# Two model blocks on one core: order of a value GEMM, pieces of the layer norms, steps of the gated attention

## The chip, the cores and the metric

One of the eight cores of a Trainium2 chip runs the whole program; the other cores stand idle. The metric is device time in microseconds (us), median of several executions. Engines: TensorE (PE, with its weight load PEld), VectorE (DVE), ScalarE (ACT), GpSimd (POOL), SyncE (SP, which issues most DMAs).

## What is computed

A sequence of 512 tokens, 1024 wide, runs through a first block (block-sparse attention beside gated linear attention, GLA, then a squared-ReLU MLP) and through two layers of a second block:

```python
# second block, per layer: deepnorm residuals around an attention and an MLP
proj = x @ w_in;  fq, fk, fv, f_logit, rq, rk, rv, rg = split(proj)
fox_out = fox_attention(fq, fk, fv, log_sigmoid(f_logit + b))       # softmax heads
ret = retention(rotary(rq), rotary(rk), rv);  ret = groupnorm(ret)  # 4 heads of 128
x = layernorm(ALPHA * x + concat(fox_out, silu(rg) * ret) @ w_out)
x = layernorm(ALPHA * x + relu(x @ w_ff1)**2 @ w_ff2)
```

All inputs are f32. Products are made of three fp32r products: each operand is split into a high and a low part.

## The kernel before

Activations lie transposed: eight tiles of 128 features by 512 tokens (`H`; split copies `P` and `Q`, each `hi` and `lo`). Weights stream from HBM in slabs into two stage buffers; `prepare()` (L253) turns one piece of 1024 columns into `wh` on ACT (L269) and `wl` on DVE (L270). `piece()` (L279) hands out the next piece and prepares ahead of it, as long as a ring slot is free. A GEMM of one piece (`gemm`, L309) is eight k steps of three matmuls (L298, L300, L301) of 512 tokens into one of four rotating PSUM banks; `gemm_tok` (L359) computes values with tokens on the partitions and goes over the four banks in turn.

Each engine runs its instructions in the order in which the Python program emits them, so that order is the schedule. Attention work is emitted in between: `tick()` (L410) follows every k step and adds `pace[0]`; at each whole number, one step of the generator at the head of `background` runs. The softmax generator (L666) takes two steps for each of 32 score tiles and calls `chore()` (L387) once in every pair; chores are small pieces of work put off by others. The rotary evacuation `ev_r` (L1483) puts off two chores for each tile, `first_half` (L1488, L1491) and `second_half` (L1496, L1499), and its bank counts as owed until the second has run. `settled(b)` (L391) runs chores until a bank's debt is gone. In a layer of the second block twelve GEMMs (L1505: rotary tiles 0 to 7 and the remaining query and key tiles) come before the value GEMM `gemm_tok(P, ev_rv)` (L1576), whose evacuation centres the values (L1511, L1513). The retention generator follows the softmax; its head 0 multiplies scores by `accq`, heads 1 to 3 by `x_dec` (L1550), which a DMA behind a reload of `H` brings (L1521, L1522).

In GLA, `gla()` (L916) runs beside 16 GEMMs of 8 ticks at a pace of 0.52. `gates(hd)` computes the decays; after the first gates three steps pass before the product L929. Three steps before the mean L992, two squares are added on DVE (L988).

`last_three` (L1257) computes the last three output tiles (5, 6, 7) ahead of a layer norm, in two halves of 256 tokens (`part(p, half, ks)`), while the norm of the first half, A, begins. `norm.late(j)` adds a tile to the running sum `accq` (L1202) and its squared deviation to `acc2`. `mean()` (L1217) and `scale()` (L1231) are matmuls with constant weights. `minus` (L1226) subtracts the mean, `times` (L1241, L1244) scales, `lows` (L1253) makes the low parts on DVE. `head(half, ks)` are the first k steps of the first three GEMMs of the next stage, by halves; the fourth GEMM comes whole after them. It is called four times: before both MLPs of the second block (LN1 of layers 0 and 1), between the layers, and at the end (`nxt` is None there: no next GEMM, and finished tiles go out by DMA).

A wait names an engine's counter and a value. `mean()` waits for `norm.acc`, the token of the last `accq` addition emitted so far, whichever half that one was for.

Of the kernel before, what the change touches and what calls it, by code (L numbers as in the profile page):

```python
# [93 lines left out]
def build(nc, xT, w_in, gate_up, w_bm, w_bg, w_out, w_up, w_down, w_in2, w_out2, w_ff1, w_ff2,  # L94
          consts, params, out, vrev, cneg):
    ctx = ExitStack()
    with ctx:
# [100 lines left out]
        for L in range(2):  # L198
# [7 lines left out]
            pair_cols(w_in2[L], 3)  # L206
            cols(w_in2[L], 1928, 2568)
            values(w_in2[L], 2568, 3080)
# [8 lines left out]
        state = {"slab": 0, "prep": 0, "use": 0, "bank": 0, "ahead": 3}  # L217
# [91 lines left out]
        def gemm(x, nk, evac, more=0):  # L309
# [3 lines left out]
            for c0 in range(0, width, 128):  # L313
# [73 lines left out]
        def chore():  # L387
            if chores:
                chores.pop(0)()

# [70 lines left out]
        t_x = []  # L461
# [5 lines left out]
        c3 = V.op(lambda e: e.memset(onev[:, :], 1.0 / 256))  # L467
        c4 = V.op(lambda e: e.memset(epsc, 1e-6))
# [37 lines left out]
        def rms_scale(t_acc, rb_use=None):  # L506
# [5 lines left out]
            t = A.op(lambda e: e.activation(rB[:, :], tB[:, :], ACT.Exp, scale=-0.5), t, rb_use)  # L512
# [153 lines left out]
        def softmax_heads(heads, vv, t_v, bias_of, finished):  # L666
# [70 lines left out]

            bias_for(0)
# [25 lines left out]
            while chores:  # L764
                chore()
                yield

# [148 lines left out]
        def gla():  # L916
# [4 lines left out]
            for _ in range(3):  # L921
                yield
            for hd in range(4):
# [67 lines left out]
                yield  # L991
                tp = PE.op(lambda e: e.matmul(banks[5][:, :], onev[:, :], sq[0][:, :], start=True,  # L992
# [14 lines left out]
        pace[0] = 0.52  # L1007
# [53 lines left out]
        finish_background()  # L1061
        for j in range(8):
# [86 lines left out]
        class Norm:  # L1149
# [50 lines left out]
            def late(self, j, sl):  # L1200

                self.acc = V.op(lambda e: e.tensor_tensor(accq[:, sl], accq[:, sl], H[:, j, sl], ALU.add),  # L1202
                                t_h[j], self.acc)
                self.deviate(j, sl)

        class Half:
# [8 lines left out]
            def mean(self):  # L1215
# [496 lines left out]
```

How the kernel before makes its waits and increments, by code:

```python
    def run(self, eng):  # L85
        for need, fn, s, inc in self.ops:
            for w, v in need:
                eng.wait_ge(w.h, v)
            ins = fn(eng)
            if s:
                ins.then_inc(s.h, inc)
# [1553 lines left out]
        @block.sync  # L1645
        def _(e):
            SP.run(e)
            e.wait_ge(s_out.h, s_out.n)
```

## Time and profile before

| | us |
|---|---|
| median of 3 runs | 2123.97 (2123.3 to 2124.76) |
| profiled execution | 2123.57 |
| its span, first to last instruction | 2121.8 |
| PE busy in the span | 2055.1 (97%) |
| DVE busy, ACT busy | 1101.9 (52%), 939.3 (44%) |
| mean granted TensorE clock | 0.995 |

The page of the profile gives busy shares; the views of the trace behind it (who waited for whom, instructions in order of time, busy time of chosen stretches with the granted clock) give the stages. Matmuls overlap, so their recorded durations are longer than their distance from start to start.

### The profile page before, as it was taken

What the parts mean: (1) busy time and instruction counts of PE and PEld (TensorE: products, weight loads), DVE (VectorE), ACT (ScalarE), POOL (GpSimd) and SP (SyncE); (2) the same over time, 40 slices, a digit from 0 to 9 for tenths busy, and PEclk for the clock granted to TensorE, in tenths of its full rate; (3) what the DMA queues carried; (4) which work ended last, traced back from release to release, by engine and by line L of the source; (5) the groups of instructions that cost most, each with busy time, mean ns of one, the idle gap of its engine ahead of it and who ended that gap; (6) DMA issues with size and microseconds to landing.
All of it is one profiled execution on the core that took longest, in us unless ns stands there. A gap on an engine that the chain in (4) does not pass through costs nothing. (4 is left out here: it accounts for less than half of the span.)

```text
span 2121.8 us, 24498 instructions
## 1 busy us (share of the span) xinstructions
PE 2055.1 (97%) x9660; PEld 1691.6 (80%) x9660; DVE 1101.9 (52%) x1795; ACT 939.3 (44%) x1513; POOL 149.4 (7%) x207
## 2 busy tenths in 40 slices
PE   8999999999999999999999999999999999999997
PEld 6888778888888888777688888888777688888886
DVE  5655556565343443576486333337676476333336
ACT  5664334335232332565557243244565347243343
POOL 0000000000000000353000000000353000000000
PEclk9999999999999999999999999999999999999999
DMA  7332213333322332632323332330632323333321
GB/s 236 95 105 64 77 60 99 121 98 120 119 91 88 100 99 61 179 100 75 114 80 102 99 103 95 100 99 21 199 91 83 114 80 100 100 99 100 99 80 40
DMA packets 201519, 211.38 MB, mean 100 GB/s; under 512 B 7803, under 2 KB 181115, under 8 KB 201404
## 3 DMA queue, kind: packets, MB, share of 16 engines
q1 hardware_dynamic: 194544, 194.13, 29.2%
q0 software_dynamic: 6352, 15.24, 2.8%
q8 instruction: 77, 1.26, 0.3%
q10 hardware_dynamic: 508, 0.43, 0.1%
q14 instruction: 38, 0.31, 0.0%
HBM read 194.55 MB, written 8.95 MB: 96 GB/s over the span
## 5 line engine op out<-in xcount | busy, mean ns | idle before, releaser
L298 PE MATMUL ps<-Phi,wh 128*128 128x512 f32 (+1 forms) x1208 | 481.1, 398 | 18.9 <-DVE Plo L448 8.7
L301 PE MATMUL ps<-Phi,wl 128*128 128x512 f32 (+1 forms) x1208 | 459.3, 380 | 0.1
L300 PE MATMUL ps<-Plo,wh 128*128 128x512 f32 (+1 forms) x1208 | 458.4, 380 | 0.0
L269 ACT ACTIVATE wh<-stage 128x1024 fp32r<-128x1024 f32 (+2 forms) x253 | 261.5, 1041 | 183.9 <-PE ps L301 167.1
L270 DVE TENSOR_TENSOR wl<-stage,wh 128x1024 fp32r<-128x1024 f32 x250 | 304.6, 1223 | 66.2 <-ACT wh L269 58.5
L298 PEld LDWEIGHTS ps<-Phi,wh 128*128 128x128 f32 x1208 | 228.4, 189 | 67.0 <-issue 19.6
L301 PEld LDWEIGHTS ps<-Phi,wl 128*128 128x128 f32 x1208 | 227.7, 188 | 44.7 <-DVE wl L270 0.8
L300 PEld LDWEIGHTS ps<-Plo,wh 128*128 128x128 f32 x1208 | 228.5, 189 | 40.8 <-issue 4.1
L298 PE MATMUL ps<-Qhi,wh 128*128 128x512 f32 (+1 forms) x680 | 256.2, 377 | 0.8 <-DVE Qlo L445 0.8
L301 PE MATMUL ps<-Qhi,wl 128*128 128x512 f32 (+1 forms) x680 | 254.4, 374 | 0.0
L300 PE MATMUL ps<-Qlo,wh 128*128 128x512 f32 (+1 forms) x680 | 254.4, 374 | 0.0
L445 DVE TENSOR_TENSOR Qlo<-f,Qhi 128x512 fp32r<-128x512 f32 x96 | 66.5, 693 | 238.8 <-ACT Qhi L444 238.8
L1120 DVE TENSOR_TENSOR H<-H,ps 128x512 f32<-128x512 f32 x72 | 49.5, 687 | 222.6 <-PE ps L301 222.6
L298 PE MATMUL ps<-Qhi,wxh 128*128 128x512 f32 (+1 forms) x408 | 150.7, 369 | 0.0
L300 PE MATMUL ps<-Qlo,wxh 128*128 128x512 f32 (+1 forms) x408 | 148.9, 365 | 0.0
L301 PE MATMUL ps<-Qhi,wxl 128*128 128x512 f32 (+1 forms) x408 | 148.8, 365 | 0.0
L298 PEld LDWEIGHTS ps<-Qhi,wh 128*128 128x128 f32 x680 | 128.1, 188 | 25.3 <-ACT Qhi L444 1.6
L300 PEld LDWEIGHTS ps<-Qlo,wh 128*128 128x128 f32 x680 | 128.1, 188 | 23.6 <-issue 1.0
L301 PEld LDWEIGHTS ps<-Qhi,wl 128*128 128x128 f32 x680 | 128.0, 188 | 22.7
L269 ACT ACTIVATE wxh<-stage 128x1024 fp32r<-128x1024 f32 x86 | 89.7, 1051 | 109.2 <-PE ps L301 104.3
L298 PE MATMUL ps<-Phi,wxh 128*128 128x512 f32 (+1 forms) x336 | 129.0, 384 | 0.0
L300 PE MATMUL ps<-Plo,wxh 128*128 128x512 f32 (+1 forms) x336 | 129.0, 384 | 0.0
(301 smaller groups left out, 2921.5 us busy)
## 6 DMA issues: line engine op xcount, KB each, us to landing
stage<-in_w_ff SPq DMA_DIRECT2D x64, 1024.0 KB, 5.4
stage<-in_w_in SPq DMA_DIRECT2D x39, 1024.0 KB, 5.3
stage<-in_w_up SPq DMA_DIRECT2D x16, 1024.0 KB, 5.3
stage<-in_w_down SPq DMA_DIRECT2D x16, 1024.0 KB, 5.2
stage<-in_w_in SPq DMA_DIRECT2D x30, 512.0 KB, 5.3
stage<-in_w_out SPq DMA_DIRECT2D x12, 1024.0 KB, 5.2
stage<-in_w_bg SPq DMA_DIRECT2D x4, 1024.0 KB, 5.4
vrev<-H SPq DMA_DIRECT2D x2, 2048.0 KB, 14.9
```

What stands on the lines that cost most here:

```text
L269: t_hi = A.op(lambda e: e.activation(hi, src, ACT.Copy), st_landed[n, part], w_free[u], sem=s_whi)
L270: t_lo = V.op(lambda e: e.tensor_tensor(lo, src, hi.bitcast(F32), ALU.subtract), st_landed[n, part], t_hi, w_free[u], sem=s_wlo)
L298: PE.op(lambda e: e.matmul(o, hi[:, k, c], x.hi[:, kx, tok], start=first, stop=False), t_hi, t_x or x.t[kx], list(waits), signal=False)
L300: PE.op(lambda e: e.matmul(o, hi[:, k, c], x.lo[:, kx, tok], start=False, stop=False), signal=False)
L301: return PE.op(lambda e: e.matmul(o, lo[:, k, c], x.hi[:, kx, tok], start=False, stop=last), t_lo, sem=s_wpe, signal=last)
L445: t2 = V.op(lambda e: e.tensor_tensor(lo, src, hi.bitcast(F32), ALU.subtract), t1, t_src, x.free, after)
L1120: t_h[j] = V.op(lambda e: e.tensor_tensor(H[:, j, :], H[:, j, :], o, ALU.add), t, t_h[j])
```

## The change

- At the start, four matmuls of constants run on PE, and the squares for the first norm's sum come three tiles behind the splits.
- `put_off` holds chores back only while the softmax generator runs (`state["turns"]`); `gemm` settles its bank as `gemm_tok` does.
- The value GEMM of the second block comes after `ev_fk(3)`, before rotary tiles 3 to 7; the slabs are reordered with it. Centring becomes a chore except for the first bank. Retention waits for the rotary tile that its head needs.
- GLA has five steps ahead of L929, one step more ahead of L992, and a pace of 0.55.
- The activation table for logarithm and exponential is loaded by name ahead of the branch GEMMs.
- `last_three` runs whole parts of the B half sooner, prepares one piece more after `part(2, 0)` and takes four GEMMs of the next stage by halves. At the end, tile 7 enters the mean and the variance through one more matmul each, and tiles 2 and 5 are finished on DVE.

```diff
                 b = next_bank()
                 o = banks[b][0:m, :]
                 for k in range(nk):
-                    t = product(o, w, k, slice(c0, c0 + m), x, k, k == 0, k == nk - 1, free[b] if k == 0 else None)
+                    t = product(o, w, k, slice(c0, c0 + m), x, k, k == 0, k == nk - 1, settled(b) if k == 0 else None)
                     tick()
...
+        def put_off(*what):
+
+            chores.extend(what)
+            while chores and not state["turns"]:
+                chore()
...
+        for _ in range(4):
+            t_idle = PE.op(lambda e: e.matmul(banks[7][:, :], ones[:, :], rB[:, :], start=True, stop=True), idle, c1)
+        free[7] = rb_free[0] = t_idle
         t_acc = None
-        for k in range(8):
-            split(P, k, H[:, k, :], [t_x[k // 2], t_prm], prm[:, V_G1 + k:V_G1 + k + 1])
+        for k in range(11):
+            if k < 8:
+                split(P, k, H[:, k, :], [t_x[k // 2], t_prm], prm[:, V_G1 + k:V_G1 + k + 1])
             if k == 0:
                 prepare()
+            k -= 3
+            if k < 0:
+                continue
...
-            for _ in range(3):
+            for _ in range(5):
...
                 sq_free[1] = t
                 yield
                 yield
+                yield
                 tp = PE.op(lambda e: e.matmul(banks[5][:, :], onev[:, :], sq[0][:, :], start=True,
...
-        pace[0] = 0.52
+        pace[0] = 0.55
...
         finish_background()
+        A.op(lambda e: e.preload_act_table_set("natural_log_exp_and_others"), signal=False)
...
+            def mean(self, rest=None):
+
                 sl, n = self.sl, self.n
-                t = PE.op(lambda e: e.matmul(banks[4][:, sl], onec[:, :], accq[:, sl], start=True, stop=True),
+                t = PE.op(lambda e: e.matmul(banks[4][:, sl], onec[:, :], accq[:, sl], start=True, stop=rest is None),
                           n.acc, free[4])
+                if rest is not None:
+                    t = PE.op(lambda e: e.matmul(banks[4][:, sl], onec[:, :], H[:, rest, sl], start=False, stop=True),
+                              t_h[rest])
...
+                while rest and n.pending:
+                    _, _, s, t_s = n.pending.pop()
+                    t = PE.op(lambda e, s=s: e.matmul(banks[5][:, sl], onec[:, :], s[:, sl], start=False, stop=True), t_s)
...
+                    if not self.keep and k in (2, 5):
+                        self.fin[k] = V.op(lambda e, k=k, g=g, b=b: e.tensor_scalar(
+                            H[:, k, sl], d8[:, k, sl], g, b, ALU.mult, ALU.add), t)
+                        continue
...
+            part(2, 0, range(8))
+            norm.add()
+            if nxt:
+                prepare()
             if last_wide:
                 narrow()
+            part(0, 1, range(8))
             A_.mean()
             A_.minus(0, 1, 2, 3)
+            part(1, 1, range(4))
             A_.scale()
             A_.minus(4, 5, 6, 7)
+            part(1, 1, range(4, 8))
             A_.times(0, 1)
+            if not nxt:
+                norm.add()
+                part(2, 1, range(8), False)
+                A_.times(2, 3)
+                B_.mean(7)
+                B_.minus(0)
+                B_.scale(True)
+                A_.times(4)
+                B_.minus(1, 2, 3, 4, 5)
+                A_.times(5, 6)
+                B_.minus(6, 7)
+                B_.times(0)
+                A_.times(7)
+                out_half(0, A_.fin)
+                for k in range(1, 8):
+                    B_.times(k)
+                    out_half(1, B_.fin, k)
+                return
             A_.lows(0)
+            A_.times(2)
+            A_.lows(1)
+            A_.times(3)
             part(2, 1, range(8))
             norm.add()
+            A_.lows(2)
+            A_.times(4)
+
+            four = [(piece(1), next_bank()) for _ in range(4)]
+
+            def step(half, k, i, w, b):
+                return product(banks[b][:, half.sl], w, k, slice(0, 128), P, k, k == 0, k == 7, free[b],
+                               tok=half.sl, t_x=half.sub[k])
 
             def head(half, ks):
+                for k in ks:
+                    for (i, w), b in four:
+                        step(half, k, i, w, b)
 
             head(A_, (0, 1))
+            A_.lows(3)
+            A_.times(5)
             B_.mean()
             A_.lows(4)
+            B_.minus(0, 1, 2)
+            A_.times(6)
+            A_.lows(5)
             head(A_, (2, 3))
             B_.scale()
+            B_.minus(3, 4)
             A_.times(7)
+            A_.lows(6)
+            B_.minus(5, 6, 7)
+            A_.lows(7)
             head(A_, (4, 5, 6, 7))
             B_.times(0)
             for k in range(1, 8):
                 B_.times(k)
                 B_.lows(k - 1)
             B_.lows(7)
+            prepare()
+            prepare()
             for k in range(8):
                 t_h[k] = [A_.fin[k], B_.fin[k]]
+                P.t[k] = [A_.sub[k], B_.sub[k]]
             rb_free[0] = B_.r
             sq_free[:] = [norm.acc2, norm.acc2]
+            head(B_, range(4))
+            for ((i, w), b), ev in zip(four, nxt):
+                for k in range(4, 8):
+                    t = step(B_, k, i, w, b)
+                P.free = t
+                release(i, t)
+                if not last_wide:
                     free[b] = ev(banks[b][:, :], t)
+            for ((i, w), b), ev in zip(four, nxt if last_wide else ()):
+                free[b] = ev(banks[b][:, :], t)
...
-            for ev in (ev_r(0), ev_fq(2), ev_fk(2), ev_r(1), ev_r(2), ev_fq(3), ev_fk(3),
-                       ev_r(3), ev_r(4), ev_r(5), ev_r(6), ev_r(7)):
+            for ev in (ev_r(0), ev_fq(2), ev_fk(2), ev_r(1), ev_r(2), ev_fq(3), ev_fk(3)):
                 gemm(P, 8, ev)
             t_rv = [None] * 4
 
             def ev_rv(b, o, t):
+                box = [OWED]
+
+                def centre():
+                    box[0] = centred(b, o, t)
+                if b:
+                    put_off(centre)
+                else:
+                    centre()
+                return box
+
+            def centred(b, o, t):
                 t1 = V.op(lambda e: e.tensor_reduce(sums[:, b, :], o.rearrange("p (h d) -> p h d", h=4), AX.X, ALU.add), t)
                 total = bass.AP(tensor=sums[:, :, :].tensor, offset=4 * b, ap=[[16, 128], [1, 4], [0, 128]])
                 t_rv[b] = V.op(lambda e: e.scalar_tensor_tensor(
                     out=rv[:, b, :].rearrange("p (h d) -> p h d", h=4), in0=total, scalar=-1.0 / 128,
                     in1=o.rearrange("p (h d) -> p h d", h=4), op0=ALU.mult, op1=ALU.add), t1, Q.free)
                 return t_rv[b]
+            gemm_tok(P, ev_rv)
...
+                    while t_r[4 + h] is None:
+                        yield
...
-            gemm_tok(P, ev_rv)
+            for j in range(3, 8):
+                gemm(P, 8, ev_r(j))
```

In the body of `last_three` only the lines after the change are shown; those before it are in the function above.

## Rows read from the trace of the kernel before

**Rows 1.** The page: busy us and share (part 1); count, busy us, mean ns (part 5).
```profile
PE 2055.1 (97%) x9660; PEld 1691.6 (80%) x9660; DVE 1101.9 (52%) x1795; ACT 939.3 (44%) x1513; POOL 149.4 (7%) x207
...
L269 ACT ACTIVATE wh<-stage 128x1024 fp32r<-128x1024 f32 (+2 forms) x253 | 261.5, 1041 | 183.9 <-PE ps L301 167.1
```

**Rows 2.** Waits of PE: line, waited for, us in total, times, longest.
```profile
PE ps L370 <- DVE x_rb L1496: 10.2, 4, 3.3
PE ps L1217 <- DVE accq L1202: 8.9, 6, 2.1
...
PE ps L1547 <- DVE x_IT L1550: 5.1, 4, 2.0
PE ps L298 <- ACT H L1244: 4.7, 3, 1.6
...
PE ps L298 <- DVE Plo L1253: 3.1, 8, 0.6
PE ps L929 <- DVE kiv L911: 2.4, 1, 2.4
PE ps L992 <- DVE sq L988: 2.3, 3, 0.8
```

**Rows 3.** Timeline of PE, start: start us, duration us, instruction, [idle before <-releaser].
```profile
13.06 0.77 PE L298 MATMUL ps<-Phi,wh 128*128 128x512 f32 x1 [0.29 <-DVE Plo L448]
...
14.91 0.63 PE L300 MATMUL ps<-Plo,wh 128*128 128x512 f32 x1
15.34 0.63 PE L301 MATMUL ps<-Phi,wl 128*128 128x512 f32 x1
...
16.63 0.39 PE L298 MATMUL ps<-Phi,wh 128*128 128x512 f32 x1
...
24.11 1.02 PE L508 MATMUL ps<-accq,onec 128*128 128x512 f32 x2
```

**Rows 4.** Stretches: length, PE, PEld, DVE, ACT, POOL busy, PEclk, DMA, GB/s.
```profile
988.95:992.35 3.40, 3.40 (x9) 2.85 (x10) 0.60 (x1) 0.00 (x0) 0.00 (x0) 0.50 0.00 0
...
1736.40:1739.85 3.45, 1.36 (x12) 1.16 (x11) 2.67 (x6) 1.21 (x2) 0.00 (x0) 1.00 0.00 0
1739.90:1743.25 3.35, 3.35 (x12) 2.99 (x13) 2.44 (x8) 1.22 (x3) 0.00 (x0) 0.50 0.00 0
```

**Rows 5.** Timeline of DVE, one rotary chore of layer 0.
```profile
988.13 0.69 DVE L1496 SCALAR_TENSOR_TENSOR x_rb<-ps,x_tab 64x512 f32<-64x512 f32 x1
```

**Rows 6.** Timeline of DVE, retention of layer 0.
```profile
1027.08 1.16 DVE L1550 TENSOR_TENSOR x_IT<-ps,x_dec 128x512 f32<-128x512 f32 x2 [7.37 <-DMA x_dec<-in_consts]
```

**Rows 7.** Timeline of PE, LN1 of layers 0 and 1, and the end.
```profile
1098.18 0.28 PE L298 MATMUL ps<-Qhi,wxh 128*128 128x256 f32 x1
...
1099.14 0.28 PE L301 MATMUL ps<-Qhi,wxl 128*128 128x256 f32 x1
...
1739.78 1.16 PE L1217 MATMUL ps<-accq,onec 128*128 128x256 f32 x2 [2.09 <-DVE accq L1202]
...
2109.11 0.70 PE L1217 MATMUL ps<-accq,onec 128*128 128x256 f32 x2 [1.51 <-DVE accq L1202]
```

**Rows 8.** Timeline of DVE, LN1 of layers 0 and 1.
```profile
1101.05 0.43 DVE L1196 TENSOR_TENSOR acc<-acc,sq 128x256 f32<-128x256 f32 x1 [0.48 <-ACT sq L1187]
1101.78 1.42 DVE L1226 TENSOR_TENSOR d<-H,muB 128x256 f32<-128x256 f32 x4
...
1737.71 1.22 DVE L270 TENSOR_TENSOR wl<-stage,wh 128x1024 fp32r<-128x1024 f32 x1 [0.59 <-ACT wh L269]
```

**Rows 9.** Timelines of PE and DVE, between the layers.
```profile
1491.06 0.28 PE L301 MATMUL ps<-Phi,wxl 128*128 128x256 f32 x1
...
1492.01 1.41 DVE L603 SCALAR_TENSOR_TENSOR f0qs<-ps,f0qs 64x512 fp32r<-64x512 f32 x2 [0.99 <-ACT f0qs L602]
```

**Rows 10.** Timelines of DVE and ACT: a copy of 256 columns; the end.
```profile
222.35 0.29 DVE L901 COPY tm<-b 128x256 f32<-128x256 f32 x1
...
2115.08 4.04 ACT L1244 ACTIVATE H<-d,prm 128x256 f32<-128x256 f32 x8 [0.74 <-DVE d L1241]
```

More of the change, by code:

```diff
@@ L206, in build @@
             pair_cols(w_in2[L], 3)
+            values(w_in2[L], 2568, 3080)
             cols(w_in2[L], 1928, 2568)
-            values(w_in2[L], 2568, 3080)
             cols(w_in2[L], 3080, 3592)
@@ L216, in build @@
         w_tok, w_free, slot = {}, [None] * 7, {}
-        state = {"slab": 0, "prep": 0, "use": 0, "bank": 0, "ahead": 3}
+        state = {"slab": 0, "prep": 0, "use": 0, "bank": 0, "ahead": 3, "turns": False}
         ring_free = [0, 1, 2, 3]
@@ L1198, in add, with late @@
                     sq_free[k % 2] = self.acc2
-            def late(self, j, sl):
-                self.acc = V.op(lambda e: e.tensor_tensor(accq[:, sl], accq[:, sl], H[:, j, sl], ALU.add),
-                                t_h[j], self.acc)
+            def late(self, j, sl, summed=True):
+                if summed:
+                    self.acc = V.op(lambda e: e.tensor_tensor(accq[:, sl], accq[:, sl], H[:, j, sl], ALU.add),
+                                    t_h[j], self.acc)
                 self.deviate(j, sl)
@@ L1227, in minus, with scale @@
                                      self.t_m, t_h[k], self.n.d[k])
-            def scale(self):
+            def scale(self, rest=False):
                 sl, n = self.sl, self.n
-                t = PE.op(lambda e: e.matmul(banks[5][:, sl], onec[:, :], acc2[:, sl], start=True, stop=True),
+                t = PE.op(lambda e: e.matmul(banks[5][:, sl], onec[:, :], acc2[:, sl], start=True, stop=not rest),
                           n.acc2, free[5])
+                while rest and n.pending:
+                    _, _, s, t_s = n.pending.pop()
+                    t = PE.op(lambda e, s=s: e.matmul(banks[5][:, sl], onec[:, :], s[:, sl], start=False, stop=True), t_s)
                 t = V.op(lambda e: e.tensor_tensor(qB[:, sl], banks[5][:, sl], qB[:, sl], ALU.subtract), t, self.q)
@@ L1283, in part @@
                     release(i, t)
-                norm.late(j, sl)
+                norm.late(j, sl, then)
             part(0, 0, range(8))
@@ L1289, in last_three @@
                 prepare()
+            part(2, 0, range(8))
+            norm.add()
+            if nxt:
+                prepare()
             if last_wide:
                 narrow()
-            part(2, 0, range(8))
-            norm.add()
-            part(0, 1, range(3))
+            part(0, 1, range(8))
             A_.mean()
             A_.minus(0, 1, 2, 3)
-            part(0, 1, (3, 4))
+            part(1, 1, range(4))
             A_.scale()
             A_.minus(4, 5, 6, 7)
-            part(0, 1, (5, 6, 7))
+            part(1, 1, range(4, 8))
@@ L1302, in last_three @@
             A_.lows(0)
-            part(1, 1, range(8))
-            for k in range(2, 5):
-                A_.times(k)
-                A_.lows(k - 1)
+            A_.times(2)
+            A_.lows(1)
+            A_.times(3)
             part(2, 1, range(8))
             norm.add()
-            if nxt:
-                two = [(piece(1), next_bank()) for _ in range(3)]
-            def head(half, ks):
-                for k in ks if nxt else ():
-                    for (i, w), b in two:
-                        t = product(banks[b][:, half.sl], w, k, slice(0, 128), P, k, k == 0, k == 7, free[b],
-                                    tok=half.sl, t_x=half.sub[k])
-                        if k == 7 and half is B_:
-                            P.free = t
-                            release(i, t)
-                return t if nxt else None
+            A_.lows(2)
@@ L1622, in build @@
             last_three(norm, alpha, V_LN1G + 8 * L, V_LN1B + 8 * L,
-                       [lambda o, t, j=j: up(j, o, t) for j in range(3)])
+                       [lambda o, t, j=j: up(j, o, t) for j in range(4)])
             norm = None
-            for j in ff(up, alpha, 3, 5):
+            for j in ff(up, alpha, 4, 5):
                 if norm is None:
```

30 lines of the change are left out of this document (7 added, 23 removed).

## The prediction

> **What bounds the kernel now.** I read the page's busy shares first: PE is busy 97% of the span [rows 1], so a change can only take away waits of PE or its slow clock. Next comes the view of PE's waits [rows 2]: the large ones are the value GEMM behind rotary chores (10.2 us in two layers), the means and first heads around the layer norms (8.9, 4.7 and 3.1), retention (5.1) and GLA (2.4 and 2.3). Then I read the stretches with the granted clock [rows 4]: twice PE falls to 0.50, the 1.2 GHz level, for 3.4 us; a fall like the first also follows the same wait in layer 1. Last come the timelines around each wait. The profiled execution took 2123.57 us, its span 2121.8; the 1.8 around it stay. The median, 2123.97, is 0.4 above it.
>
> **The start.** PE runs without a gap from 13.06, behind DVE's split of tile 1 [rows 3]. The copy of the first square stands ahead of that split; moved three tiles back, it frees up to the 0.3 us that PE waits there. At first matmuls follow each other every 0.43 us (14.91 to 15.34), later every 0.227 (33 of them from 16.63 to 24.11). The 42 from 13.06 to 24.11 took 11.05 us, at full speed 42 x 0.227 = 9.5: the slow part costs 1.5. The four constant matmuls are f32, two passes each; L508 shows 0.43 a pass at full speed [rows 3], so 8 passes at half speed are 6.9 us, begun behind DVE's first memsets and done about when PE's first operand is there; before that PE has nothing to do, so they cost nothing, whatever they bring. But after them PE has only six matmuls until 13: it stands most of that time, as it did ahead of the fall at 1739.9 (1.36 us busy in 3.45) [rows 4]. So the clock may fall again. The gain lies between 0 and 1.8; I take 1.0, the middle.
> The Trainium skill, page "TensorE: Matmul & The Clock Gate", calls the slow level the default that activity releases (section "What's actually happening"); by that alone the term would be -1.8 and the forecast 2109.0. Its section "HAM oscillation — how this bites in real kernels" says that a wait between bursts brings the slow level back; by that it would be -0.3 and 2110.5. The row at 1739.9 agrees with the second.
>
> **GLA.** A step comes every 1/0.55 ticks of three matmuls, 1.82 x 0.68 = 1.24 us of PE (1.31 before). Two more steps give L929's operand 2.5 us for a wait of 2.4; one more gives L988 1.24 for waits of at most 0.8 [rows 2]. Both could go: -4.7. Every other chain loses 0.07 us a step, and what ends next to nothing today may show; I take -4.3, bounds -5 and -2.5. The steps are 65 now (59 before); 128 ticks give 70, so none is left over. The table load by name and what it moves on ACT cost nothing: no wait of PE in rows 2 lies at the Ln that it serves.
>
> **Rotary and values.** Ahead of the value GEMM four tiles' chores are owed now, and its second round of banks runs them in a burst: 10.2 us of waits, 5.1 a layer [rows 2]. The second wait ends in the fall of the clock, 3.4 us at half speed, 1.7 lost [rows 4]. Put behind `ev_fk(3)`, the value GEMM finds banks whose debts are paid: -6.8 a layer. What is late next? Chores run once in two steps, at 0.52 a tick 2.1 in a GEMM, and every tile adds two; three centrings of 1.4 us come on top. I count three chores, 3 x 1.4 = 4.2 us of DVE (two operations of 0.69 each) [rows 5], left when tile 7's GEMM ends. They stand ahead of retention's first products on DVE, where today the last centrings and the last head stand: that wait (part of L1547's 5.1 [rows 2]) stays. SP's queue moves too: the reload of `H` waits for the last chore, and `x_dec` is behind it. DVE already stands 7.37 us for `x_dec` [rows 6]; I take it 0.8 later (0 to 1.2), all of it PE's wait. Denser chores in the five GEMMs cost 0.7 in small waits (0 to 2). Net -5.3 a layer, -10.6 in all; bounds -14 and -7.
>
> **The norms before a next GEMM (three).** PE's work is the same, the fourth GEMM's in halves instead of whole: 24 more matmuls of 0.12 us (8 steps in 0.96) [rows 7] in each half. So the time moves by the sum of waits: 8.9 + 4.7 + 3.1 [rows 2] less the 1.5 at the end, 15.2 for three, 5 each; those 1.5 and the 2.09 below stand in [rows 7]. Three things speak against its going. First, `part(0, 1)` now comes whole ahead of `A_.mean()`, and `norm.acc` is then the addition of the B half's tile 5, so the mean of A waits for a number that it doesn't need. Second, the extra `prepare()` puts a 1.22 us split, behind 1.04 us for its high part on ACT [rows 1], on DVE in between; that split already made the wait of 2.09 in layer 1 [rows 8]. In LN1 of layer 0 the last sum of A starts on DVE at 1101.05 [rows 8]; the split then runs from about 1102.1 to 1103.3, tile 5's sum is ready at 1104.1, while PE, 15 matmuls after 1099.4 [rows 7], is at the mean at 1101.2: 2.9 us of wait. Third, from there DVE has some 20 operations of 0.335 (four in 1.42 [rows 8]) and the hops over ACT, about 9.5 us, until the first low part, and PE has 48 x 0.12 + 0.7 and the hop: it waits 2.2 more. With 1 in small pieces it is 6 against 5. From DVE's side, the earlier cover gives 1.4 back. I take -0.5, -0.5 and, as layer 1 already has its fall, -1.2: -2.2 in all, bounds -6 and +4.
> One new wait is sure: between the layers all four evacuations come after the last matmul, and the thin forget GEMM reuses the first one's bank. Matmuls end at about 1491.3, L603's two operations at 1493.4 [rows 9]: +2.1 (1.5 to 2.5).
>
> **The end.** The mean of A again waits for tile 5 of B, without a split: +1.1 for PE. Four finishing operations go from ACT to DVE, 0.29 (a copy of 256) [rows 10] to 0.42 each [rows 8]: +1.2 to 1.7 on the engine that is last then. The eight finishes on ACT, 4.04 us, end behind DVE's last operation today [rows 10], and that lag goes; one `accq` and one `acc2` addition (0.34 each) go too, but DVE waits for tile 7 with `times` behind it. +1.8, bounds 0 and +2.8.
>
> **Sum.** -1.0 - 4.3 - 10.6 - 2.2 + 2.1 + 1.8 = -14.2: span 2107.6, an execution like the profiled one 2109.4, the median 2109.8.
>
> **Rivals.**
> Norms pay: if tile 5's sum and the extra split fit beside PE (the split's ACT half done early), the waits fall from 5 to about 2 in each norm: -10 instead of -2.2, and the end +0.5. -1.0 - 4.3 - 10.6 - 10 + 2.1 + 0.5 = -23.3: 2100.7. For it: four GEMMs cover more than three. Against it: both lie on DVE's in-order path.
> Rotary gives part of it back: more chores are left than I count, or `x_dec` and a new fall of the clock cost 5 a layer. -2 a layer: -7.6, 2116.4. For it: DVE waits on `x_dec` already.
> The reordering doesn't do what it says: the key tile's evacuation just ahead of the value GEMM takes the place of the rotary burst, and rotary gains nothing: -3.6, 2120.4. Against it: only one bank, with 4.1 us of matmuls before it is needed.
> Slower: the burst moves to the end of tile 7's GEMM, where nothing but `step_background` stands until retention begins. With all five tiles left DVE has 14 us to do, PE none, and the clock falls: 15.7 a layer against 6.8 won. -3.6 + 2 x 8.9 = +14.2: 2138. It decides from about 8.6 us left a layer, three tiles. Against it: two chores a GEMM do run.
>
> **How the numbers follow.** Forecast 0.58 (its own range 2104 to 2115), norms pay 0.15, rotary gives back 0.17, nothing from rotary 0.05, slower 0.05. About 0.2%, 4.2 us, is what a measurement of this kernel can tell from no change. Faster by more: 0.58 + 0.15 + 0.14 = 0.87; within: 0.08 (the fifth case and the weak end of the third); slower: 0.05. The range goes from the norms' case to beyond the third: 2101 to 2118.
>
> **What would show it.** Right: no L370 wait on L1496, clock 1.00 around the value GEMM; L929 and L992 gone from PE's waits; longer L1217 waits on L1202 in LN1; a thin GEMM (L333) waiting 2 us for L603; at the start a clock that rises before 8 us and may fall. Wrong: L1217 without a wait (norms pay), or an L1547 wait over 4 us (rotary gives back).

## The result and the profile after

The changed kernel took 2111.1 us (median of four executions, 2108.95 to 2113.26) where the kernel before took 2123.64 beside it: a ratio of 0.9941, 95% interval 0.9925 to 0.9956. Predicted were 2109.8 and a range of 2101 to 2118. The profiled execution took 2113.26, its span 2110.7, 11.1 less than the span before; the forecast for it was 14.2 less. It is the slowest of the four, with a mean granted clock of 0.990 where the two at 2109.0 have 0.994.

The time falls into place when the same matmul is looked up in both traces and its start compared. Seven matmuls of before stand as marks, at 24.11 (the first mean), 339.57 (behind GLA), 1073.58 (in front of the last GEMM tiles ahead of LN1 of layer 0), 1155.55 (behind that norm), 1537.57 (softmax of layer 1, so the norm between the layers and the thin GEMM lie ahead of it), 1711.86 and 1795.54 (around LN1 of layer 1). Each cell is the change of the shift from one mark to the next, in us, profiled execution against profiled execution (negative is time gained); "spans" is the sum. The column of layer 0 begins behind GLA and so holds the rest of the first block too. The kernels below "changed" are the experiments, and the table is used for them too. A row rests on one execution; oldval's is the slowest of ten, 5.7 above its median.

| kernel | start | GLA | layer 0 to retention's end | LN1, layer 0 | between layers | layer 1 to retention's end | LN1, layer 1 | end | spans |
|---|---|---|---|---|---|---|---|---|---|
| predicted | -1.0 | -4.3 | -5.3 | -0.5 | +1.6 | -5.3 | -1.2 | +1.8 | -14.2 |
| changed | -0.0 | -5.4 | -6.9 | +1.2 | +1.4 | -6.2 | +1.6 | +3.3 | -11.1 |
| again | -0.3 | -5.4 | -7.9 | +1.2 | +1.0 | -5.2 | +1.6 | +3.3 | -11.7 |
| oldval | +1.0 | -5.4 | -1.9 | +2.2 | +2.5 | -1.0 | +0.5 | +3.3 | +1.2 |
| oldnorm | +0.0 | -5.4 | -6.9 | +0.0 | -0.8 | -6.2 | +1.0 | +0.0 | -18.2 |
| token | -0.2 | -5.4 | -7.7 | +1.0 | +0.8 | -5.0 | -0.2 | +3.1 | -13.5 |
| toksplit | -0.5 | -5.4 | -7.6 | +0.9 | +2.8 | -5.3 | +0.6 | +3.1 | -11.4 |
| early | -0.4 | -5.3 | -7.8 | +0.7 | +3.8 | -5.8 | +0.2 | +3.3 | -11.3 |
| hold | -0.3 | -5.4 | -7.7 | +1.3 | +3.1 | -6.1 | +1.4 | +3.2 | -10.5 |
| hold2 | -0.7 | -5.4 | -7.8 | -0.1 | +1.2 | -6.1 | -0.5 | +3.3 | -16.1 |
| ret | -0.4 | -5.3 | -6.9 | +1.2 | +1.8 | -5.4 | +1.3 | +3.6 | -10.2 |
| swap | -0.3 | -5.4 | -9.2 | +2.1 | +2.0 | -5.2 | +1.6 | +3.2 | -11.2 |
| combo | -0.4 | -5.4 | -10.3 | +1.6 | +0.1 | -9.3 | +1.0 | +0.0 | -22.8 |
| last | -0.1 | -5.4 | -10.0 | -1.1 | +7.8 | -9.3 | -1.6 | -0.0 | -19.7 |

So GLA and the rotary stages gave 18.5 and the norms, the thin GEMM and the end took 7.5 back; the start gave nothing. The waits of PE in the changed kernel (line, waited for, us in total, times, longest) show the first half of that:

```profile
PE ps L1237 <- DVE accq L1221: 9.8, 4, 4.1
PE ps L1613 <- DVE x_IT L1616: 6.6, 2, 3.3
PE ps L298 <- ACT H L1274: 4.7, 3, 1.8
PE ps L333 <- DVE f0qs L617: 2.2, 1, 2.2
...
PE ps L728 <- DVE stat L716: 1.0, 3, 0.4
```

Against [rows 2] the 10.2 at the value GEMM and the 4.7 of GLA are gone. The means (L1217 before, L1237 now) wait about as long as before, but in four waits instead of six, the longest 4.1 instead of 2.1. Retention's wait (L1547, now L1613) grew from 5.1 to 6.6. The thin GEMM's wait is new. The gaps between PE's matmuls, added up over each trace, went from 55.9 to 32.5, 23.4 less, and the span got only 11.1 shorter. 4.7 of the difference lie ahead of the first mean, where the constant matmuls fill a gap and the mean comes no sooner; behind it the gaps are 18.7 shorter. Most of the rest is the clock. The stretches of the changed kernel in which it was 0.50 (length, PE, PEld, DVE, ACT, POOL busy, PEclk, DMA, GB/s):

```profile
13.20:16.60 3.40, 3.40 (x10) 2.62 (x9) 3.40 (x7) 3.40 (x7) 0.00 (x0) 0.50 1.05 386
...
1003.10:1009.90 6.80, 5.64 (x14) 4.57 (x15) 3.23 (x6) 0.00 (x0) 0.00 (x0) 0.50 0.72 223
1091.85:1095.25 3.40, 3.40 (x15) 3.22 (x16) 1.93 (x6) 1.22 (x3) 0.00 (x0) 0.50 0.95 277
1460.55:1463.95 3.40, 3.40 (x18) 3.40 (x17) 2.88 (x9) 2.15 (x5) 0.00 (x0) 0.51 0.00 0
1487.85:1491.25 3.40, 3.31 (x8) 1.49 (x9) 3.27 (x5) 3.28 (x6) 2.63 (x5) 0.51 1.06 400
1641.45:1644.85 3.40, 3.40 (x9) 2.32 (x8) 0.56 (x3) 0.00 (x0) 0.00 (x0) 0.51 0.98 349
1726.75:1733.55 6.80, 5.88 (x23) 5.52 (x24) 4.14 (x13) 1.93 (x5) 0.00 (x0) 0.50 0.50 157
```

Before there were three such stretches of 3.4 [rows 4] (the third, in layer 1, is like the first), besides the last microseconds; its start was slow too, with matmuls 0.43 apart until 15.34 [rows 3]. Now there are seven. The first belongs to the start. The other six have 27.2 us, and each lies at or behind a wait of PE: retention's (1003 and 1641), the means' (1092 and 1727), the first scaled tile's (1460), the thin GEMM's (1488). PE was busy 25.0 us in these six at half speed, about 12.5 lost against 5 before.

What was to be seen by the prediction: no wait on the second rotary product, and no fall of the clock around the value GEMM, which now ends at 962 (where it stood before, from 975 to 1000, the clock is 1.00; before 0.93); L929 and L992 gone; the thin GEMM waiting 2.2 for L603's line (now L617); a fall of the clock at the start. All are there. Long waits on L1202 (now L1221) are there too. No retention wait reaches 4.

### The profile page after: what moved, and what is told of

The parts are those of the page before. It is cut to its first block and busy times, and to the rows that moved or that the text cites. A ratio compares the mean times of both kernels' runs of the same rounds, so it can differ in the third digit from the quotient of the medians.

```text
span 2110.7 us, 24662 instructions
## 1 busy us (share of the span) xinstructions
PE 2064.2 (98%) x9744; PEld 1702.1 (81%) x9744; DVE 1101.9 (52%) x1798; ACT 921.5 (44%) x1498; POOL 149.0 (7%) x207
## 5 line engine op out<-in xcount | busy, mean ns | idle before, releaser
L301 PEld LDWEIGHTS ps<-Qhi,wl 128*128 128x128 f32 x680 | 128.0, 188 | 22.8
L298 PE MATMUL ps<-Phi,wxh 128*128 128x512 f32 (+1 forms) x368 | 136.7, 371 | 0.0
L300 PE MATMUL ps<-Plo,wxh 128*128 128x512 f32 (+1 forms) x368 | 136.7, 371 | 0.0
```

Of the source, the lines that this page charges most:

```text
L298: PE.op(lambda e: e.matmul(o, hi[:, k, c], x.hi[:, kx, tok], start=first, stop=False), t_hi, t_x or x.t[kx], list(waits), signal=False)
L300: PE.op(lambda e: e.matmul(o, hi[:, k, c], x.lo[:, kx, tok], start=False, stop=False), signal=False)
L301: return PE.op(lambda e: e.matmul(o, lo[:, k, c], x.hi[:, kx, tok], start=False, stop=last), t_lo, sem=s_wpe, signal=last)
```

## The experiments

All are edits of the changed kernel; times are medians with the ratio to the kernel before, run beside them.

**again.** No edit.

> The changed kernel itself, for its spread. Its first four executions stood at 2109.0, 2109.0, 2113.2 and 2113.3, with mean granted clocks of 0.994, 0.994, 0.991 and 0.990. Theory 1 (PE's clock falls behind some of its waits, not always the same ones): again two groups some 4 us apart, the slower with the lower clock, none between, and a profile of the faster group has fewer stretches at 0.50 than the nine counted in the first profile. Theory 2 (plain scatter): times spread evenly between 2109 and 2113 at one clock.

Measured: 2111.94, ratio 0.994 (0.9928 to 0.9953), single executions at 2108.74, 2110.13, 2111.94, 2111.96 and 2112.57 with mean clocks of 0.991 to 0.993. There are no two groups. But the clock does differ between executions of one kernel at one place. The two retention stretches in this profile:

```profile
1002.50:1009.30 6.80, 5.33 (x23) 3.93 (x24) 3.51 (x7) 0.10 (x1) 0.00 (x0) 1.00 0.61 203
1637.25:1644.05 6.80, 5.77 (x14) 4.57 (x15) 3.10 (x6) 0.00 (x0) 0.00 (x0) 0.50 0.68 235
```

In layer 0 the same wait of 3.28 is followed by no fall, and PE then stands 1.32 at head 1; the stage is 1.0 us better than in the first profile. In layer 1 the fall lasts twice as long as there, and the stage is 1.0 worse. A single profile's stage with such a wait is therefore uncertain by about 1 us.

**oldval.** The value GEMM and its slabs back in their old place, centring at once:

```diff
-                if b:
+                if False:
                     put_off(centre)
...
-            gemm_tok(P, ev_rv)
+            for j in range(3, 8):
+                gemm(P, 8, ev_r(j))
             t_fox, t_dec = [], [t_dec0]
...
-            for j in range(3, 8):
-                gemm(P, 8, ev_r(j))
+            gemm_tok(P, ev_rv)
             while not t_fox:
```

> The changed kernel with the value GEMM back behind rotary tiles 3 to 7, its four centrings at once, and the slabs in the old order. Theory 1 (the two traces' shift over these stages, 6.9 in the first layer and 8.7 in the second): 2126 to 2127, with the waits on the second rotary product back at some 10 us. Theory 2 (the prediction's term): 10.6 slower, 2121.7. Theory 3 (the gain is not from the order but from the chores' rule): the time stays at 2111.

Measured: 2120.24, ratio 0.998 (0.9971 to 0.9989); 8.3 slower than the run of "again" beside it. The wait is back whole:

```profile
PE ps L370 <- DVE x_rb L1549: 10.2, 4, 3.3
```

By the table the order is worth 5.0 to 6.0 in layer 0 (-1.9 against -6.9 and -7.9) and 4.2 to 5.2 in layer 1 (-1.0 against -5.2 and -6.2). The table's row is a slow execution: it has a fall of the clock at 977.7, behind the first wait of layer 0, that the kernel before doesn't have, so layer 0's part may be 1 to 2 too high. By the medians the order is worth some 8 to 9 in both layers together. It is the change's main gain. Theory 2 comes nearest. Without the order layer 0 still gains 1.9 and layer 1 1.0. That part was in no term of the sum; small waits of PE went, the most of them in the softmax, one line in the kernel before:

```profile
PE ps L714 <- DVE stat L702: 3.8, 7, 0.7
```

Of these 3.8, 1.1 are left here and 1.0 in the changed kernel, so it wasn't the order that took them. The likeliest cause is the chores' new rules (`put_off` and `settled`); neither was tried alone.

**oldnorm.** `Norm`, `Half` and `last_three` of the kernel before, with their calls: three GEMMs by halves, no extra split, the old end.

> The changed kernel with the norms' code of the kernel before: three GEMMs of the next stage by halves, no extra split, the old ending. Theory 1 (by the shift between the two traces, the norm before each MLP came 1.2 and 1.6 later, the one between the layers with the thin GEMM 3.9, the end 3.2: 9.9 in all): about 10 faster than the changed kernel, 2101. Theory 2 (the prediction's terms: norms -2.2, thin GEMM +2.1, end +1.8): 1.7 faster, 2109.4. Theory 3 (the lost clock comes with the stage, whichever way it is cut): no change, 2111.

Measured: 2103.56, ratio 0.9906 (0.9893 to 0.992), 8.4 faster than "again". Theory 1 comes nearest, its gain some 1.5 too high. The norms' part of the change made the kernel slower: 1.2 in LN1 of layer 0, 2.2 between the layers, 0.6 in LN1 of layer 1, 3.3 at the end, 7.3 by the table. Why, the next runs ask.

**token.** The mean of half A waits for its own sum:

```diff
+            own = norm.acc
             part(0, 1, range(8))
-            A_.mean()
+            A_.mean(acc=own)
```

> The changed kernel with one token changed: the mean of half A waits for A's own last sum and not for tile 5 of half B. Theory 1 (a false wait): PE's waits on that sum ahead of the three norms, 2.8, 1.9 and 4.1, fall below 1 each, the clock falls behind them go, and the kernel is 4 to 8 us faster, 2103 to 2107. Theory 2 (VectorE's order sets the pace, not PE): tile 5's three operations and the split stand on DVE ahead of A's subtractions as before, so what PE no longer waits at the mean it waits at the scale or at the first low part: within 1 us of 2111.

Measured: 2108.67, ratio 0.9931 (0.9917 to 0.9944); with "again" at 2111.94 the gain is within the spread of single executions. In the changed kernel this is LN1 of layer 0, DVE:

```profile
1087.46 0.42 DVE L1221 TENSOR_TENSOR accq<-accq,H 128x256 f32<-128x256 f32 x1
...
1089.65 1.23 DVE L270 TENSOR_TENSOR wxl<-stage,wxh 128x1024 fp32r<-128x1024 f32 x1 [0.52 <-ACT wxh L269]
1090.80 0.41 DVE L1303 SCALAR_TENSOR_TENSOR H<-H,ps 128x256 f32<-128x256 f32 x1
1091.25 0.42 DVE L1221 TENSOR_TENSOR accq<-accq,H 128x256 f32<-128x256 f32 x1
```

and PE:

```profile
1091.72 1.14 PE L1237 MATMUL ps<-accq,onec 128*128 128x256 f32 x2 [2.83 <-DVE accq L1221]
...
1101.70 0.36 PE L298 MATMUL ps<-Phi,wh 128*128 128x256 f32 x1 [1.56 <-ACT H L1274]
```

A's own sum ends at 1087.9; the mean waits for the one at 1091.25, behind the split, as the prediction had it (2.9 forecast, 2.83 measured). With the token changed the mean starts at 1087.82 and doesn't wait. Then, on PE:

```profile
1099.35 0.55 PE L298 MATMUL ps<-Phi,wh 128*128 128x256 f32 x1 [4.77 <-ACT H L1274]
```

4.77 in one wait, where 2.83 and 1.56 stood. ScalarE shows why:

```profile
1087.67 1.04 ACT L269 ACTIVATE wxh<-stage 128x1024 fp32r<-128x1024 f32 x1
1091.13 0.42 ACT L1205 ACTIVATE sq<-d 128x256 f32<-128x256 f32 x1 [2.42 <-DVE d L1198]
1091.45 0.37 ACT L1242 ACTIVATE muB<-ps 128x256 f32<-128x256 f32 x1
```

The copy of the mean to SBUF (L1242) stands behind the square of tile 5 of half B, and that behind the split on DVE. The mean is there at 1088.4 and is copied at 1091.45. Theory 2, by the waits: the false wait was real, but taking it away frees none of PE's waits, since the same two pieces of work stand ahead of the mean's copy by order. The median is 2.3 below the 2111 of theory 2, which allowed 1. The table puts 1.8 of its row's gain on LN1 of layer 1 (-0.2 against +1.6), where the waits sum up to the same (one of 5.45 for 4.07 and 1.31) and a fall of 6.8 us is in both; why the stage is shorter there wasn't tried.

**toksplit.** The same, with the extra split moved behind the second tile of half B.

> The run with the mean's own token, and besides the extra split of a weight piece moved from ahead of the mean to behind the second tile of half B, ahead of the first scalings. Theory 1 (the split lengthens VectorE's chain by 1.2 and ScalarE's by 1.0 only where it stands ahead of the mean): PE's waits on the first scaled tile, 4.8, 3.8 and 5.5 with the token alone, fall by 1.2 to 2 each; 3 to 5 us faster than that run, 2104 to 2106. Theory 2 (the split is on the same chain wherever it stands before the first low part): waits and time as with the token alone, 2108 to 2109.

Measured: 2110.73, ratio 0.993 (0.9912 to 0.9949). The waits on the first scaled tile are 4.75, 4.66 and 5.45, 14.9 in all against 14.0 with the token alone. The waits are those of theory 2: the split is on the chain to the first low part there as well.

**early.** Four GEMMs by halves stay, but the mean of half A goes between the k steps of tile 5 again, as in the old code, and the split behind the first scalings:

```diff
-            if nxt:
-                prepare()
...
-            part(0, 1, range(8))
+            part(0, 1, range(3) if nxt else range(8))
             A_.mean()
             A_.minus(0, 1, 2, 3)
-            part(1, 1, range(4))
+            if nxt:
+                part(0, 1, (3, 4))
+            else:
+                part(1, 1, range(4))
             A_.scale()
             A_.minus(4, 5, 6, 7)
-            part(1, 1, range(4, 8))
-            A_.times(0, 1)
+            if nxt:
+                part(0, 1, (5, 6, 7))
+                A_.times(0, 1)
+                A_.lows(0)
+                part(1, 1, range(8))
...
             A_.times(3)
+            prepare()
             part(2, 1, range(8))
```

> The changed kernel with four GEMMs by halves as it has them, but in the norms before a next GEMM the mean and the scale of half A stand again between the k steps of tile 5 of half B, ahead of that tile's operations on VectorE and ScalarE, and the extra split stands behind the first scalings. The end is left as changed. Theory 1 (tile 5's three operations and the split, on VectorE and ScalarE ahead of the mean's copy, are what the norms lost): the waits at the means get below 1, those on the first scaled tile below 1, and the norms are 1 to 3 each better than with the old code: 2104.5 less 3 to 9 of norms but with the end's 3.2 left in, 2100 to 2105. Theory 2 (four GEMMs by halves don't cover more than three): the norms are as with the old code, 2106 to 2108.

Measured: 2113.35, ratio 0.995 (0.9935 to 0.9964): no faster than the changed kernel, and slower than either theory. In LN1 of layer 0 the wait at the mean fell from 2.83 to 0.85, and then PE stands here:

```profile
1099.69 0.39 PE L298 MATMUL ps<-Phi,wxh 128*128 128x256 f32 x1 [3.15 <-ACT wxh L269]
1100.95 0.58 PE L301 MATMUL ps<-Phi,wxl 128*128 128x256 f32 x1 [0.76 <-DVE wxl L270]
```

Now the split itself is late: the fourth GEMM needs a weight piece that three don't. So the split can't stand last either.

**hold.** Constant matmuls ahead of six of PE's waits, in the norms for example

```diff
+            for _ in range(holds.pop(0) if nxt else 0):
+                PE.op(lambda e: e.matmul(banks[4][:, halves[0]], onec[:, :], cB[:, halves[0]], start=True, stop=True),
+                      norm.t_c, free[4])
             A_.mean()
```

> The changed kernel with constant matmuls in PE's order ahead of six of its waits, a little shorter than each wait: 10, 6 and 14 (256 columns) ahead of the means of half A in the three norms, 6 (512 columns) at retention's third product in both layers, 4 ahead of the thin GEMM between the layers. They work on nothing that is used. Theory 1 (each fall of the clock costs its own length): the falls behind these waits go and the kernel is 8 to 10 us faster, 2102 to 2104. Theory 2 (in the norms the half clock is covered, since VectorE's chain sets the next wait): only retention (about 2 a layer) and the thin GEMM (1.6) give time back, 2106 to 2107, and in the norms PE's wait on the first scaled tile grows by what the mean's fall took. Theory 3 (short constant matmuls don't hold the clock): falls and time as in the changed kernel, 2111 to 2112.

Measured: 2113.27, ratio 0.9943 (0.9928 to 0.9958). The numbers of matmuls were wrong: each is two passes, as in the prediction's own row for L508 [rows 3], and one had been counted. They outlasted the waits (retention's third product started at 1005.92 instead of 1003.97 in "again"), so this run can't decide between the theories.

**hold2.** The same with 6, 4 and 9 ahead of the means, 3 at retention, 2 ahead of the thin GEMM.

> The run with constant matmuls again, with their number taken from their measured length (0.43 for one of 256 columns, 0.86 for one of 512: two passes each), since those of the first run outlasted the waits: 6, 4 and 9 ahead of the three means, 3 at retention in both layers, 2 ahead of the thin GEMM. Theory 1 (a fall costs its own length): 8 to 10 us faster than the changed kernel, 2102 to 2104. Theory 2 (what a fall takes at a norm or at retention is time that PE would wait a little later for VectorE or for x_dec): only the thin GEMM's 1.6 and part of retention's is won, 2108 to 2111, and waits of 1.3 for x_dec at head 1 stand where the falls were.

Measured: 2107.88, ratio 0.9925 (0.9911 to 0.994), 3 to 4 faster than the changed kernel. Of the falls between 17 us and the end one is left (at 1459). The two MLP norms in this run:

```profile
1085.00:1102.00 17.00, 14.97 (x110) 14.02 (x109) 13.24 (x36) 8.27 (x18) 0.00 (x0) 1.00 0.19 62
1720.00:1737.00 17.00, 14.97 (x102) 13.46 (x100) 13.39 (x36) 8.12 (x17) 0.00 (x0) 1.00 0.21 62
```

and the same in the changed kernel (PE's busy time above includes the constant matmuls):

```profile
1086.00:1103.00 17.00, 12.61 (x88) 12.00 (x87) 12.54 (x33) 7.21 (x16) 0.00 (x0) 0.90 0.21 62
1722.00:1739.00 17.00, 11.62 (x70) 10.88 (x69) 11.90 (x29) 5.99 (x13) 0.00 (x0) 0.80 0.20 63
```

With the clock held these norms cost -0.1 and -0.5 instead of +1.2 and +1.6: the fall is worth 1.3 and 2.1 there. Retention gains nothing (-7.8 and -6.1, in the range of the two profiles of the changed kernel), since waits of 1.3 at head 1 stand where the falls were. Between the layers nothing is won either (+1.2 against +1.4 and +1.0), though the thin GEMM's fall is gone. The truth lies between theories 1 and 2: PE was busy 21.6 us in the five falls that went, at half speed some 11 lost, and about 4 came back.

**ret.** Three empty steps before head 0's third product, pace 0.68:

```diff
                         if j % 2:
                             next(norm, None)
                             yield
+                        for _ in range(3 if h == 0 and j == 1 else 0):
+                            yield
...
-            pace[0] = 0.58
+            pace[0] = 0.68
```

> The changed kernel with three empty steps in retention between the second and the third product of head 0, so that PE works on the gate's GEMM while VectorE ends the last rotary chores, and a pace of 0.68 instead of 0.58 there. Theory 1 (the wait of 3.3 is only a matter of order): it goes in both layers, with the clock's falls behind it: 8 to 10 us faster, 2102 to 2104. Theory 2 (what is late next is x_dec, or the end of retention): 1 to 3 of each 3.3 come back as a wait at head 1 or at the norms of the heads, 2106 to 2109.

Measured: 2112.2, ratio 0.994 (0.9926 to 0.9955): nothing. The wait moved to head 1 and to x_dec:

```profile
PE ps L1613 <- DVE x_IT L1616: 5.3, 4, 2.2
```

**swap.** The transfer of `x_dec` ahead of the reload of `H`.

> The changed kernel with the transfer of x_dec ahead of the reload of H in SyncE's queue: it no longer waits for the last rotary chore. Theory 1 (x_dec is late next): VectorE's wait of 8.8 for x_dec gets 3 to 6 shorter, and PE's wait of 1.3 at head 1, which the second profile of the changed kernel shows in layer 0, goes; up to 1.3 a layer, 2109 to 2111. Theory 2 (behind the wait at head 0 PE is late enough): no PE wait changes, 2111 to 2112.

Measured: 2109.86, ratio 0.9929 (0.9913 to 0.9945), within the spread. VectorE's wait for x_dec (17.7 in two layers) is gone altogether, PE's 3.3 at head 0 stays in both. In layer 0 no fall of the clock follows it here, as in "again", and the 1.32 at head 1 that stood there is gone; the stage is some 1.2 better than in "again". In layer 1 it is no better. So theory 1's wait went where it had stood, a gain too small for the median to show.

**combo.** The edits of oldnorm, ret and swap together.

> The changed kernel with three of the edits above together: the old norms, the three empty steps in retention, x_dec ahead of the reload of H. Theory 1 (the empty steps won nothing only because x_dec was late next, and x_dec alone little because the first wait hid it): the 3.3 and its fall go in both layers, 8 to 10 us less than the 2103.6 of the old norms alone, 2094 to 2096. Theory 2 (each edit moves its wait on to the next operation): 2102 to 2104.

Measured: 2099.98, ratio 0.988 (0.9863 to 0.9897), single executions from 2095.66 to 2101.03. What ret and swap didn't give alone they give together: -10.3 and -9.3 in the two attention stages, and

```profile
PE ps L1578 <- DVE x_IT L1581: 1.1, 2, 0.6
```

is what remains of retention's waits, with no fall of the clock behind them. The median is 3.6 below oldnorm's, less than the 8 of theory 1; the profiles' spans differ by 4.5. Against oldnorm's profile the two attention stages gain 6.6, and 1.6 goes again in LN1 of layer 0: its waits are those of oldnorm, but here the clock falls behind one of 1.55 (at 1097.6) and there it doesn't. It is the fastest kernel of this study, faster than the kernel before and the changed one.

**last.** `early` with the split behind A's last subtractions, the old end, `ret` and `swap`, the thin GEMM in bank 7, no constant matmuls at the start.

> The changed kernel with what the runs so far point to, each in a stage of its own. Norms before a next GEMM: four GEMMs by halves, the mean of half A between the k steps of tile 5 as in the old code, the extra split behind the last subtractions of half A (in the run before it stood behind the first scalings, and PE waited 3.2 for ScalarE's half of it and 0.8 for VectorE's). End: the old order. Thin GEMM between the layers: bank 7. Retention: three empty steps, x_dec ahead of the reload. Start: without the four constant matmuls, the squares shifted as changed. Norms, theory 1 (three causes were named rightly: tile 5's operations, the split's place, the thin GEMM's bank): waits under 2.5 in each norm against 4.4 to 6.3 with the old code, no wait of the thin GEMM: 6 to 10 less than the 2100.0 of the run with old norms, empty steps and x_dec, 2090 to 2094. Theory 2 (VectorE's chain has no room for the split anywhere before the head): waits of 4 to 6 in each norm, 2099 to 2102. Start, theory 1 (the constant matmuls bring nothing): the first norm's mean within 0.7 of 24.1, as in the other profiles; theory 2: 1 to 1.5 later.

Measured: 2103.7, ratio 0.9897 (0.9881 to 0.9914), above the times of both theories. The two norms ahead of MLPs are the best of all runs (-1.1 and -1.6), with waits of 3.4 each. Between the layers the split came too late again, +7.8:

```profile
1456.67 1.04 ACT L269 ACTIVATE wh<-stage 128x1024 fp32r<-128x1024 f32 x1
```

is its ScalarE half, and PE waits for it:

```profile
1457.76 0.58 PE L298 MATMUL ps<-Phi,wh 128*128 128x256 f32 x1 [5.67 <-ACT wh L269]
```

There the call for the split now stands behind `narrow()`, which takes three of the seven ring slots away; by the kernel's text no slot is free then, the call does nothing, and the piece is split only when the head asks for it; the trace shows the late split, not the cause. The thin GEMM in its own bank no longer waits, but the next GEMM does, 2.4 for a weight piece behind the evacuations. At the start the first operand's matmul is at 9.22 and the first mean at 23.99, with the constant matmuls at 23.4 to 24.1 in eleven profiles and 25.07 in oldval's: they bring nothing that can be seen.

## Why the prediction was right, and where it was not

The time fell inside the range and 1.3 from the forecast, but the sum owes that to errors of both signs: by the table four stages came out 3.8 better than forecast and the other four 7.0 worse, in an execution 2.2 above the median. That these errors nearly cancel in the median is luck.

**The start** (-1.0, measured 0.0). The clock rose early and fell again at 13.2, for 3.4 us, as the step said it might. The forecast took the middle between two cases; both profiles of the changed kernel show the case that the row at 1739.9 [rows 4] spoke for. The Trainium skill says the same, page "TensorE: Matmul & The Clock Gate", section "HAM oscillation — how this bites in real kernels": a wait between bursts brings the slow level back. The trace agrees (PEclk 0.50 from 13.20 to 16.60), and the term by that reading, -0.3, was the better one.

**GLA** (-4.3, measured -5.4, in all thirteen profiles 5.3 to 5.4). Mechanism right: both waits went. The 0.4 taken off for chains that would lose time didn't come, and some 0.7 came beyond the 4.7 of waits; PE was idle 4.7 of the 100 us from 220 before and 0.05 after, so these 0.7 are in the matmuls' distances and not in waits. Their cause wasn't tried.

**Rotary and values** (-10.6, measured -13.1 in the two columns). The order itself is worth 4 to 6 a layer by oldval, 5.3 were forecast. Its steps held. Three chores are left when tile 7's GEMM ends, six operations of DVE, and retention's first product stands behind them; x_dec comes later (VectorE waits 8.83 for it instead of 7.37 [rows 6]):

```profile
999.42 0.69 DVE L1549 SCALAR_TENSOR_TENSOR x_rb<-ps,x_tab 64x512 f32<-64x512 f32 x1
...
1002.91 0.69 DVE L1552 TENSOR_TENSOR x_rqk<-x_rqk,x_rb 128x512 f32<-128x512 f32 x1
1003.52 1.15 DVE L1616 TENSOR_TENSOR x_IT<-ps,accq 128x512 f32<-128x512 f32 x2
...
1015.16 1.16 DVE L1616 TENSOR_TENSOR x_IT<-ps,x_dec 128x512 f32<-128x512 f32 x2 [8.83 <-DMA x_dec<-in_consts]
```

The term that failed is "denser chores cost 0.7 in small waits": small waits fell instead. PE's waits at the softmax line shown under oldval went from 1.7 to 0.3 in each layer, and 0.65 a layer that PE waited for ScalarE's `x_wk` in retention (L1530) is gone as well. These rows were not listed. The prediction priced retention's wait without a fall of the clock; there is one in most profiles, and ret and hold2 show that behind it x_dec was due anyway.

**The norms** (-2.2 for three; measured +1.2 and +1.6 in LN1, where -0.5 and -1.2 were forecast). Between the layers oldnorm puts 2.2 on the norm and the thin GEMM together, 1.6 forecast; the column's +1.4 is less, since oldnorm has -0.8 there without them, and where that comes from wasn't tried. The waits came nearly as worked out: in LN1 of layer 0 2.83 at the mean (2.9) and 1.56 at the first scaled tile (2.2), and in sum 0.8, 0.7 and 0.3 less than before in the three norms, where 0.5, 0.5 and 1.2 less were forecast. The term that was missing is the clock: the change makes one wait of 2 to 4 us out of several of 0.2 to 2.1, and in both profiles of the changed kernel the clock falls behind it in both LN1, for 3.4 and 6.8 us (before only in layer 1, for 3.4). hold2 puts 1.3 and 2.1 on these falls, which turns -0.1 and -0.5 into +1.2 and +1.6. The prediction counted such falls at the start and in rotary, and here only the one that layer 1 already had. The named cause was half right as well: the mean did wait for a sum that it doesn't need, but by token that wait only moves. What sets the norm is the order on VectorE and ScalarE, with tile 5's operations and the extra split ahead of the mean's copy: with these moved, in last, the two LN1 cost -1.1 and -1.6. "Norms pay" fell by the sign that it was given: L1217 has its wait.

**The thin GEMM** (+2.1, measured 2.2 [rows 9]). Right. A fall of the clock that wasn't counted comes with it, but taking that fall away won nothing there (hold2).

**The end** (+1.8, measured +3.3, outside the bounds of 0 and 2.8). oldnorm takes all 3.3 back. The step that was missing is the order on ScalarE ahead of the copy of half B's mean. ScalarE in the changed kernel's end:

```profile
2096.66 0.60 ACT L1274 ACTIVATE H<-d,prm 128x256 f32<-128x256 f32 x1 [0.70 <-DVE d L1267]
2097.16 0.36 ACT L1242 ACTIVATE muB<-ps 128x256 f32<-128x256 f32 x1
...
2106.37 1.09 ACT L1274 ACTIVATE H<-d,prm 128x256 f32<-128x256 f32 x2 [0.36 <-DVE d L1267]
```

and VectorE:

```profile
2097.55 0.43 DVE L1243 TENSOR_TENSOR qB<-muB,cB 128x256 f32<-128x256 f32 x1 [0.94 <-ACT muB L1242]
```

The copy of half B's mean stands behind ScalarE's finish of tile 3 of half A, which waits for VectorE; PE has the mean ready at 2095.8:

```profile
2095.10 0.70 PE L1240 MATMUL ps<-H,onec 128*128 128x256 f32 x2 [0.39 <-DVE H L1307]
```

Its copy starts 1.4 later, and VectorE idles 0.94 for it. The prediction followed what is queued on VectorE and not what stands ahead of the copy on ScalarE. Besides, from ScalarE's last finish (2107.5) to the end of the span it is 3.2 us, 2.7 before [rows 10]; why the last transfer takes longer wasn't tried.

**Open.** Whether the old norms between the layers with those of "last" ahead of the MLPs, in combo, would be some 5 us faster still, as the table suggests (-1.1 and -1.6 against +1.6 and +1.0), wasn't tried.

## What to carry to other kernels

A wait that is taken out of one engine's order shows its worth only after what stands ahead of the same result on the other in-order engines has been read as well: in token and ret a wait went and the next operation had it. Price a wait with the clock behind it: several short waits and one long one of the same sum cost the same by the wait view, and 1.3 to 2.1 us different here. Two edits whose gain alone is lost in the spread may be worth doing together, when one uncovers what the other removes (ret and swap, in the attention stages of combo and last).

## What was not expected of the hardware

The granted clock is not the same from one execution to the next: behind the same wait of 3.28 in layer 0's retention it was 0.50 for 6.8 us in one profile of the changed kernel and 1.00 in the other, and nine executions of that kernel lie between 2108.7 and 2113.3. Holding the clock with constant matmuls works (a mean of 0.996 to 0.997 in hold2, 0.990 to 0.994 without), but it gave back only some 4 of the roughly 11 us that the falls had taken.
